# Positions of five mixer steps in a hand-ordered encoder layer (one core)

## The chip, the cores and the metric

One core of a Trainium2 chip runs the whole layer. The metric is the device time of one execution in microseconds (us). Engines in the profile's names: PE is the matrix engine (PEld its weight loads), DVE the vector engine, ACT the scalar engine, POOL the general-purpose engine whose queue issues some DMAs, SP the engine whose queue issues the weight loads.

## The reference, cut to what matters

One residual block over 256 tokens and a model width of 2048, in float32. "..." marks what is left out.

```
h = rms_norm(x, attn_norm_w)
hq, hf, hi, hg, c_q, c_kv, k_r = split(h @ w_in)      # 4 x 1024 and 512, 512, 64 columns
# head group A (8 heads of 128): gated linear recurrence
q = silu(hq);  f = lb + (1 - lb) * sigmoid(hf);  k = 1 - f;  b = cumsum(log f) inside chunks of 64
o_a = rms_norm(q . k . exp(b_t - b_s) against hi, plus the state carried over chunks) * silu(hg)
# head group B (8 heads): latent attention
q = rms_norm(c_q) @ w_uq;  kv = rms_norm(c_kv) @ w_ukv      # per head norm, rotary on 64 columns
o_b = softmax(mask(q k^T / sqrt(192))) v
x = x + concat([o_a, o_b]) @ w_out
...
x = x + (silu(gate) * up) @ w_down      # gate, up = rms_norm(x) @ w_gate_up, width 5632
```

## The kernel before, in words

**Granules.** All weights stream from HBM in pieces ("granules") of up to 128 x 1024 elements, in one fixed order. SP loads granule g into one of four slots of `raw` as soon as the old content of the slot has been split. ACT rounds it to `w_hi` (L793), DVE takes the difference `w_lo = raw - w_hi` (L1134), and PE multiplies it: tokens-high by `w_hi`, tokens-low by `w_hi`, tokens-high by `w_lo` (L1766, L1769), for two blocks of 128 tokens. A full granule of 2 x 512 columns is 12 matmuls of 512 columns; those of `w_uq` are 12 matmuls of 384 columns. The mixer has 137 granules. Their order is: three blocks of latent columns (granules 0 to 24), then hq 0 (25 to 32), uq 0 (33, 34), hf 0 (35 to 42), ukv 0 (43, 44), hi 0 (45 to 52), uq 1 (53, 54), hg 0, ukv 1, hq 1 (65 to 72), uq 2 (73, 74), ukv 2 (75, 76), hf 1 (77 to 84), uq 3 (85, 86), ukv 3 (87, 88), hi 1 (89 to 96), hg 1 (97 to 104), then w_out. The feed-forward part follows in loops of its own.

**Steps.** Everything else in the mixer is a *step*: an entry of the list that `schedule()` (L215) writes by hand, with a *position*, which is a granule's number. Each of PE, DVE and ACT walks the granules in order in its own instruction stream. At position g, PE first executes its part of the steps of g, then multiplies granule g (L1933). ACT and DVE first convert granule g + 3 and then execute their parts of the steps of g (L1061, L1680). Steps of one position keep the order in which the list names them. No engine reorders anything: whatever waits at the head of a stream holds back all that stands behind it, conversions too. A position is therefore an order within three queues, not a time.

**The steps that matter here.**
- `lat_in`, `lat_a`, `lat_b`, `swap lat`: normalize a latent (i = 0 for q, 1 for kv), transpose its 32 x 32 blocks on DVE, and let POOL's DMAs carry the blocks through HBM and back. `lat_t i n` splits the landed transpose: ACT writes `mT_hi` (L843), DVE then writes `mT_lo` (four instructions, L1155). Granule 33, the first of uq 0, waits for `lat_t 0 1`.
- `angles` (DVE, 19 small instructions, L1201 to L1225) and `sines` (ACT: it loads the table for Sin, waits for the angles, computes, and loads the next table, L866 and L832) make the rotary tables.
- `lb_a/b/c`: the lower bounds of the forget gate, on DVE and ACT. `kr_b`: rotation of the rotary key.
- `q_a`, `q_b`, `k_a`, `k_b`: squares of a block of heads on ACT (L815), mean on DVE, a root on ACT (L826, L828), scaling and rotation on DVE into `stage` (L1319, L1190 to L1195). `q_t`, `k_t`: PE transposes `stage` into two side banks (L1820, L1824) and ACT copies them out.
- `scores`, `softmax`, `probs_t`, `attend`: the attention of one head.
- `turn`: transposes of hq and hf; ACT writes `hqT`, `hkT` and the logarithms `logT` (L955). `scan g` is the cumulative sum on DVE (four instructions, L1374). `lev_a g l` makes the exponents of level l on DVE (L1386, L1387 for level 1), `lev_b` is two exponentials on ACT (L964, L965) and two products on DVE (L1405, L1406), `pairs g l` is PE's matmuls of the level (L1870 for level 1) and a masked copy on DVE.
- `o_a g`: PE computes the output of four heads in two side banks (L1913, L1914; 24 matmuls of 128 columns), ACT takes eight sums of squares (L815), DVE the mean (L1460). `o_b g`: a root on ACT, then DVE scales and gates the banks (eight instructions, L1470, four for each bank). `swap o 0`: transpose and DMAs as above.

**Side banks.** Four PSUM banks are dealt out in turn to all uses of PE's side work, in the order of the list: use n gets bank n modulo 4 (L1772), and PE waits until the use four before it has been read out:

```
pe.wait_ge(s_given[USES[n - SIDE][1]], GIVEN[n - SIDE])
```

A use of `o_a` counts as read out only by DVE's part of `o_b`. In the order before, the uses around it are: `attend 3` in bank 0, `q_t 2` in banks 1 and 2, `o_a 0` in banks 3 and 0, `k_t 2` in banks 1 and 2, `scores 4` in bank 3.

Of the kernel before, what the change touches and what calls it, by code (L numbers as in the profile page):

```python
# [101 lines left out]
END = {blk[:2]: 1 + max(g for g, x in enumerate(GRANULES) if x[0] == b) for b, blk in enumerate(BLOCKS)}  # L102
# [112 lines left out]
def schedule():  # L215

    s = [(FIRST, ("vec", 0))] + [(at, ("x", p)) for p, at in enumerate(X_TURNED)]  # L220
    s += [(2 * c + 3, ("sq1", c)) for c in range(4)]
    s += [(10, ("r1a",)), (11, ("r1b",)), (19, ("vec", 1))]

    s += [(END[("lat", n)] + 2 * (n == 0), ("lat_in", n)) for n in range(3)]
    for i in range(2):
        e = END[("lat", i + 1)]
        s += [(e + 1, ("lat_a", i)), (e + 2, ("lat_b", i)), (e + 2, ("swap", "lat", i))]
        s += [(e + 13 - 2 * i + n, ("lat_t", i, n)) for n in range(2)]
    e = END[("lat", 2)]
    s += [(e + 1, ("kr_a",)), (e + 4, ("angles",)), (e + 5, ("sines",)), (e + 9, ("kr_b",))]  # L230

    s += [(e + 7, ("lb_a", 0)), (e + 13, ("lb_b", 0)), (e + 15, ("lb_c", 0))]
    e = END[("ukv", 2)]
    s += [(e + 2, ("lb_a", 1)), (e + 3, ("lb_b", 1)), (e + 5, ("lb_c", 1))]


    for j in range(HEADS // 2):
        q, k = END[("uq", j)], END[("ukv", j)]
        early = j >= 2
        s += [(q - early, ("q_a", j)), (q - 1 if early else q + 1, ("q_b", j)), (q + 4, ("q_t", j))]  # L240
        early = j == 2
        s += [(k - early, ("k_a", j)), (k - 1 if early else k + 1, ("k_b", j)), (k + 4, ("k_t", j))]
        for h in (2 * j, 2 * j + 1):

            p = k + 5 + (j > 1) + (7 if j == 2 else 3) * (h % 2)
            s += [(p, ("scores", h)), (p + 1, ("softmax", h)), (p + 3 + (h == 6), ("probs_t", h)),
                  (p + 5 + (h in (4, 6)), ("attend", h))]

    for g in range(2):
        late = 5 * g  # L250
        e = END[("hf", g)]
        s += [(END[("hq", g)], ("hq", g)), (e - g, ("hf_a", g))]
        s += [(END[("hq", g)] + 1, ("swap", "hq", g))]
        s += [(e + 2 - 4 * g, ("turn", g, 0, t)) for t in range(NT)] + [(e + 3 + 3 * g, ("turn", g, 1, t)) for t in range(NT)]
        p = e + 5 + late
        s += [(p, ("scan", g))]
        for l in range(1, LEVELS + 1):
            s += [(p, ("lev_a", g, l)), (p + 1, ("lev_b", g, l)), (p + 4, ("pairs", g, l))]
            p += 4 if l == 1 else 3
        s += [(p + 1, ("join_a", g)), (p + 2, ("join_b", g)), (p + 5, ("join7", g)), (p + 6, ("join_c", g)),  # L260
              (p + 8, ("join8", g))]
        s += [(END[("hi", g)], ("hi", g)), (END[("hg", g)], ("hg", g))]

        p = max(p + 10, END[("hg", g)] + 2, END[("ukv", 2)] + 3)
        s += [(p, ("o_a", g)), (p + 1, ("o_b", g))] + [(p + 1, ("swap", "o", g))] * (g == 0)

        p = max(p + 4 - g, END[("ukv", HEADS // 2 - 1)] + 6)
        s += [(p, ("o_t", g, 0)), (p, ("o_t", g, 1))]

    for c in range(4):  # L270
        s += [(END[("out1", c)], ("out1", c)), (END[("out2", c)], ("out2", c)), (END[("out2", c)] + 1, ("sq2", c))]
    s += [(END[("out2", c)] + 2, ("x2", c, n)) for c in range(4) for n in range(2)]
    e = END[("out2", 3)]
    s += [(e + 3, ("r2a",)), (e + 4, ("r2b",))]
    return sorted(s, key=lambda x: x[0])


SCHEDULE = schedule()


# [1817 lines left out]
```

## Time and profile before

| | us |
|---|---|
| median of 3 runs (1129.71 to 1131.63) | 1129.92 |
| the profiled execution's own time | 1129.12 |
| its span, first to last instruction | 1127.4 |
| PE busy | 1112.1 (99% of the span) |
| PEld busy | 935.8 (83%) |
| DVE busy | 894.0 (79%) |
| ACT busy | 642.0 (57%) |
| mean granted PE clock | 0.998 of full |

The span is what the trace shows; 1.7 us of the execution's own time lie around it. A busy share is an average over the whole program; the change lies in the mixer, which is about the first 430 us. The sixteen DMA engines move 208 GB/s on average.

### The profile page before, as it was taken

Reading aid. Unit: us, or ns where it says so; the run is one execution under the profiler, and the core shown is the slowest. Engines: PE = TensorE matmul, PEld = TensorE weight load, DVE = VectorE, ACT = ScalarE, POOL = GpSimd, SP = SyncE. Lnnn points to the kernel's source line nnn. Section 1 sums busy time; section 2 is a strip of 40 time slices with the busy share of each in tenths; the row PEclk is TensorE's granted clock in tenths of the full one; section 3 lists DMA queues with packets and bytes.
Section 4 is the critical chain, followed back from the end, with each engine's and each line's share of the span. In section 5 each row is a group of like instructions: output and inputs, shape, how many; then the busy total and the mean of one; then the engine's idle time right before and its main releaser. Section 6 shows DMA issues by size and latency. Waiting matters only on the chain.

```text
span 1127.4 us, 15411 instructions
## 1 busy us (share of the span) xinstructions
PE 1112.1 (99%) x5225; PEld 935.8 (83%) x5225; DVE 894.0 (79%) x1217; ACT 642.0 (57%) x909; POOL 64.8 (6%) x159
## 2 busy tenths in 40 slices
PE   8999999999999999999999999999999999999998
PEld 7978888887888888888888888888888888888887
DVE  5679786588776567688888988988988879889777
ACT  7557866567764556454554554554554555555553
POOL 3010000010000000000010010010000010000000
PEclk9999999999999999999999999999999999999999
DMA  8687455556554455667677677677677786666665
GB/s 266 190 268 223 147 153 167 156 175 206 179 193 167 155 184 180 192 215 233 225 232 235 222 233 238 219 232 240 217 238 225 231 273 220 208 206 195 209 194 168
DMA packets 108919, 234.23 MB, mean 208 GB/s; under 512 B 8601, under 2 KB 19650, under 8 KB 108610
## 3 DMA queue, kind: packets, MB, share of 16 engines
q1 hardware_dynamic: 101346, 209.30, 58.0%
q0 software_dynamic: 7216, 24.12, 7.3%
q8 instruction: 29, 0.48, 0.2%
q14 instruction: 24, 0.20, 0.0%
q10 hardware_dynamic: 304, 0.14, 0.0%
HBM read 220.94 MB, written 12.58 MB: 207 GB/s over the span
## 4 chain that ended last, share of the span: by engine, by line
PE 90%; DVE 5%; ACT 2%; DMA 1%; issue 1%; POOL 0%; DVEq 0%; ACTq 0%; POOLq 0%; SPq 0%
PE side L1984 24%; PE main L1766 19%; PE side L1986 12%; PE main L1769 9%; PE side L1956 4%; PE side L1958 4%; PE side L1957 4%; PE main L1958 3%; PE main L1957 3%; PE main L1956 3%; DMA raw<-in_w_in 1%; DVE w_lo L1134 1%; PE side L1882 1%; PE side L1789 1%; ACT w_hi L793 1%
## 5 line engine op out<-in xcount | busy, mean ns | idle before, releaser
L1027 ACT CAST w_hi<-raw 128x1024 fp32r<-128x1024 f32 (+1 forms) x245 | 241.6, 990 | 173.0 <-PE side L1984 102.4
L1605 DVE TENSOR_TENSOR w_lo<-raw,w_hi 128x1024 fp32r<-128x1024 f32 (+1 forms) x245 | 275.5, 1139 | 22.3 <-ACT w_hi L1027 22.0
L1134 DVE TENSOR_TENSOR w_lo<-raw,w_hi 128x1024 fp32r<-128x1024 f32 (+3 forms) x156 | 178.4, 1153 | 105.5 <-ACT w_hi L793 103.4
L793 ACT CAST w_hi<-raw 128x1024 fp32r<-128x1024 f32 (+3 forms) x156 | 153.7, 993 | 139.8 <-PE main L1766 131.2
L1766 PE MATMUL main<-w_hi,hT_hi 128*128 128x512 f32 (+2 forms) x448 | 173.3, 388 | 2.1 <-DVE hT_lo L1155 0.9
L1769 PE MATMUL main<-w_hi,hT_lo 128*128 128x512 f32 (+2 forms) x448 | 169.1, 378 | 0.0
L1984 PE MATMUL side<-w_hi,hT_hi 128*128 128x512 f32 x400 | 155.6, 389 | 0.0
L1986 PE MATMUL side<-w_hi,hT_lo 128*128 128x512 f32 x400 | 155.6, 389 | 0.0
L1766 PE MATMUL main<-w_lo,hT_hi 128*128 128x512 f32 (+2 forms) x448 | 114.8, 378 | 0.0
L1984 PE MATMUL side<-w_lo,hT_hi 128*128 128x512 f32 x400 | 106.9, 389 | 0.0
L1766 PEld LDWEIGHTS main<-w_hi,hT_hi 128*128 128x128 f32 x448 | 84.8, 189 | 15.9 <-DVE hT_lo L1155 1.9
L1769 PEld LDWEIGHTS main<-w_hi,hT_lo 128*128 128x128 f32 x448 | 84.8, 189 | 13.0
L1766 PEld LDWEIGHTS main<-w_lo,hT_hi 128*128 128x128 f32 x448 | 83.0, 189 | 14.1
L1984 PEld LDWEIGHTS side<-w_lo,hT_hi 128*128 128x128 f32 x400 | 75.1, 188 | 15.6
L1984 PEld LDWEIGHTS side<-w_hi,hT_hi 128*128 128x128 f32 x400 | 75.1, 188 | 15.6
L1986 PEld LDWEIGHTS side<-w_hi,hT_lo 128*128 128x128 f32 x400 | 75.1, 188 | 15.6
L1984 PE MATMUL side<-w_hi,aT_hi 128*128 128x512 f32 x208 | 80.9, 389 | 0.0
L1986 PE MATMUL side<-w_hi,aT_lo 128*128 128x512 f32 x208 | 80.9, 389 | 0.0
L1605 DVE TENSOR_TENSOR w_lo<-last_two,w_hi 128x1024 fp32r<-128x1024 f32 x36 | 44.1, 1225 | 45.7 <-ACT w_hi L1027 45.7
L1027 ACT CAST w_hi<-last_two 128x1024 fp32r<-128x1024 f32 x36 | 37.9, 1052 | 59.9 <-PE side L1984 59.9
L1027 ACT CAST w_hi<-first_two 128x1024 fp32r<-128x1024 f32 x36 | 38.0, 1056 | 58.8 <-PE side L1984 58.8
L1766 PE MATMUL main<-w_hi,mT_hi 128*128 128x512 f32 (+1 forms) x160 | 62.7, 392 | 2.8 <-DVE mT_lo L1155 2.7
(293 smaller groups left out, 1836.0 us busy)
## 6 DMA issues: line engine op xcount, KB each, us to landing
raw<-in_w_gate_up SPq DMA_DIRECT2D x176, 512.0 KB, 4.8
raw<-in_w_down SPq DMA_DIRECT2D x88, 512.0 KB, 4.4
raw<-in_w_in SPq DMA_DIRECT2D x64, 512.0 KB, 4.4
raw<-in_w_out SPq DMA_DIRECT2D x32, 512.0 KB, 3.7
raw<-in_w_in SPq DMA_DIRECT2D x15, 384.0 KB, 4.4
squares<-hiddenT POOLq DMA_DIRECT2D x11, 512.0 KB, 5.2
hiddenT<-squares POOLq DMA_DIRECT2D x44, 128.0 KB, 4.9
raw<-in_w_ukv SPq DMA_DIRECT2D x8, 512.0 KB, 3.7
```

The lines of the kernel that those rows point to most:

```text
L793: copy(w_hi[:, slot, 0:n], raw[:, slot, 0:n]).then_inc(s_hi, 1)
L1027: copy(w_hi[:, n % RING, 0:cols], src).then_inc(s_hi, 1)
L1134: tt(w_lo[:, slot, 0:n], raw[:, slot, 0:n], w_hi[:, slot, 0:n].bitcast(F32), ALU.subtract)\
L1605: tt(w_lo[:, n % RING, 0:cols], src, w_hi[:, n % RING, 0:cols].bitcast(F32), ALU.subtract)\
L1766: m = matmul(banks[t][:, 0:cols], hi[:, at[n], tok], rhs, start=(part == "hi" and k == k_first), stop=(part == "lo" and k == last))
L1769: matmul(banks[t][:, 0:cols], lo[:, at[n], tok], rhs, start=False, stop=False)
L1789: m = transpose(ps[:, at:at + P], where[:, t, (k + n) * P:(k + n + 1) * P], ident[:, :])
L1956: matmul(bank, hi, big, start=first, stop=False)
L1957: matmul(bank, lo, big, start=False, stop=False)
L1958: return matmul(bank, hi, small, start=False, stop=last)
L1984: m = matmul(bank, hi, rhs, start=False, stop=(part == "lo" and (t, half) in last))
L1986: matmul(bank, lo, rhs, start=False, stop=False)
```

## The change

Five kinds of step get other positions; no instruction is added or taken away.

| step | position before | after |
|---|---|---|
| `lat_t 0 0`, `lat_t 0 1` | 30, 31 | 28, 29 |
| `scan 0`; `lev_a 0 1` | 48; 48 | 46; 47 |
| `o_a 0`; `o_b 0` and `swap o 0` | 80; 81 | 77; 78 |
| `scan 1`; `lev_a 1 1` | 95; 95 | 93; 94 |

`angles` stays at 29 and stands behind `lat_t 0 1` there; `sines` stays at 30. `scan 0` stands last at 46, behind `k_b 0` and the turns. At 78 `attend 3` stands ahead of `o_b 0`; at 79 stand `lb_a 1` and `q_t 2`. The side banks are dealt anew by the same rule: `o_a 0` gets banks 0 and 1, `attend 3` bank 2, `q_t 2` banks 3 and 0, `k_t 2` banks 1 and 2, `scores 4` bank 3.

```diff
     for i in range(2):
         e = END[("lat", i + 1)]
         s += [(e + 1, ("lat_a", i)), (e + 2, ("lat_b", i)), (e + 2, ("swap", "lat", i))]
-        s += [(e + 13 - 2 * i + n, ("lat_t", i, n)) for n in range(2)]
+        s += [(e + 11 + n, ("lat_t", i, n)) for n in range(2)]
...
         p = e + 5 + late
-        s += [(p, ("scan", g))]
+        s += [(p - 2, ("scan", g))]
         for l in range(1, LEVELS + 1):
-            s += [(p, ("lev_a", g, l)), (p + 1, ("lev_b", g, l)), (p + 4, ("pairs", g, l))]
+            s += [(p - (l == 1), ("lev_a", g, l)), (p + 1, ("lev_b", g, l)), (p + 4, ("pairs", g, l))]
             p += 4 if l == 1 else 3
...
-        p = max(p + 10, END[("hg", g)] + 2, END[("ukv", 2)] + 3)
+        p = max(p + 10, END[("hg", g)] + 2, END[("ukv", 2)])
         s += [(p, ("o_a", g)), (p + 1, ("o_b", g))] + [(p + 1, ("swap", "o", g))] * (g == 0)
```

## Rows read from the trace of the kernel before

**Rows 1.** PE's waits over the program: who, for whom, us in total, times, longest.

```profile
PE main L1766 <- DVE mT_lo L1155: 2.7, 1, 2.7
PE side L1870 <- DVE E L1406: 1.1, 1, 1.1
PE side L1843 <- DVE probs L1356: 0.8, 1, 0.8
PE main L1766 <- issue: 0.8, 1, 0.8
PE side L1833 <- DVE E L1470: 0.6, 1, 0.6
```

**Rows 2.** Timeline, PE, granules 32 to 39: start, us, engine, line, operation [idle before].

```profile
81.59 1.07 PE L1766 MATMUL main<-w_lo,hT_hi 128*128 128x512 f32 x4
85.31 0.45 PE L1766 MATMUL main<-w_hi,mT_hi 128*128 128x384 f32 x1 [2.65 <-DVE mT_lo L1155]
...
88.11 0.53 PE L1766 MATMUL main<-w_hi,mT_hi 128*128 128x384 f32 x1
...
102.08 0.60 PE L1820 MATMUL side<-ident,stage 128*128 128x128 f32 x4
```

**Rows 3.** Windows: stretch, PE, PEld, DVE, ACT, POOL busy, granted clock, DMA.

```profile
88.00:91.00 3.00, 3.00 (x13) 3.00 (x13) 1.58 (x3) 2.81 (x3) 0.00 (x0) 0.64 0.62 177
```

**Rows 4.** Timeline, DVE, positions 29 to 36.

```profile
80.63 0.95 DVE L1134 TENSOR_TENSOR w_lo<-raw,w_hi 128x768 fp32r<-128x768 f32 x1
...
84.12 1.13 DVE L1155 SCALAR_TENSOR_TENSOR mT_lo<-hbT,vec_cols,mT_hi 128x128 fp32r<-128x128 f32 x4
...
94.57 1.18 DVE L1134 TENSOR_TENSOR w_lo<-raw,w_hi 128x1024 fp32r<-128x1024 f32 x1
...
101.08 0.28 DVE L1195 TENSOR_TENSOR stage_r<-rot 128x128 f32<-128x128 f32 x1
```

**Rows 5.** Timeline, ACT, from `sines` to the end of `hq 0`.

```profile
81.09 1.28 ACT L832 ACT_TABLE_LOAD   x1
...
83.12 0.90 ACT L843 ACTIVATE mT_hi<-hbT,vec_cols 128x256 fp32r<-128x256 f32 x2
...
89.80 1.05 ACT L793 CAST w_hi<-raw 128x1024 fp32r<-128x1024 f32 x1
```

**Rows 6.** Timeline, PE, the first granules of the program.

```profile
6.41 0.52 PE L1769 MATMUL main<-w_hi,hT_lo 128*128 128x384 f32 x1
...
11.83 0.34 PE L1769 MATMUL main<-w_hi,hT_lo 128*128 128x384 f32 x1
```

**Rows 7.** Timeline, ACT, the last logarithm of `turn 0`.

```profile
128.18 0.59 ACT L955 ACTIVATE logT<-side 128x512 f32<-128x512 f32 x1
```

**Rows 8.** Timeline, DVE, from position 47 to `lev_a 0 1`.

```profile
131.25 2.36 DVE L1134 TENSOR_TENSOR w_lo<-raw,w_hi 128x1024 fp32r<-128x1024 f32 x2 [3.42 <-ACT w_hi L793]
133.53 2.43 DVE L1374 TENSOR_TENSOR_SCAN hbT<-keep,logT 128x256 f32<-128x256 f32 x4
...
136.65 1.22 DVE L1387 SCALAR_TENSOR_TENSOR E<-E,hbT 128x1024 f32<-128x1024 f32 x1
```

**Rows 9.** Timeline, ACT, conversions and the squares of `o_a 0` (the first of 8).

```profile
234.52 2.01 ACT L793 CAST w_hi<-raw 128x1024 fp32r<-128x1024 f32 x2
...
243.59 0.28 ACT L815 ACTIVATE junk<-side 128x128 f32<-128x128 f32 x1
...
246.72 1.04 ACT L793 CAST w_hi<-raw 128x1024 fp32r<-128x1024 f32 x1
```

**Rows 10.** Timeline, DVE, the scaling of `o_b 0`.

```profile
249.58 2.16 DVE L1470 SCALAR_TENSOR_TENSOR E<-side,stat,hgate 128x128 f32<-128x128 f32 x8
```

**Rows 11.** Timeline, PE: `q_t 2`, the end of `o_a 0`, the start of `o_a 1`.

```profile
234.63 0.60 PE L1820 MATMUL side<-ident,stage 128*128 128x128 f32 x4
...
240.94 0.39 PE L1914 MATMUL side<-hv,hS 128*128 128x128 f32 x2
...
378.95 1.05 PE L1914 MATMUL side<-hv,hS 128*128 128x128 f32 x8
```

## The prediction

> **What bounds the kernel now.** PE is busy for 99% of the span, so the change can win only where PE waits, and each new wait of PE costs its full length. I read the list of PE's waits first [rows 1]: 2.7 us for the low half of the first latent, once; 1.1 us for the products of level 1, once; 0.6 us for a side bank held by `o_b 0`; 0.8 us for the softmax of head 4; and 0.8 us under "issue". The timeline tells that the last is granule 89, the first of hi 1, whose main banks `q_b 3` reads late. All lie in the mixer. The timeline of PE then gives the pace: the four matmuls of the row at 81.59 take 1.07 us of which the last alone is 0.39, so 512 columns start every 0.227 us and a full granule takes 2.72 us; one of `w_uq` takes 2.08. What a side step costs PE is the distance between the main matmuls around it, less this pace: `q_t` or `k_t` 0.57, `attend` 0.58, `scores` 1.12, `o_a` 2.59, and the first main matmul behind any of them 0.11 more.
>
> The wait at 85.31 is dearer than it reads [rows 2]. PE stops for 2.65 us and resumes at full pace; 1.5 us later the pace halves, as the 0.53 us matmul at 88.11 shows, and the granted clock of the window from 88 to 91 is 0.64 of full [rows 3]: 1.2 GHz up to 90.1, 2.4 after. The two granules then take 5.84 us where 4.16 would do. So granule 35 starts at 91.15 instead of 86.65: 2.82 for the wait and 1.68 for the clock.
>
> **First latent's splits ahead of the angles.** In the changed order DVE does the first split after the conversion that ends at 74.87, the second after the next one. ACT has their high halves by 72.1 and 74.05; the transposed latent has landed before 70. Four L1155 instructions hold DVE 1.05 us [rows 4], so `angles` begins and ends 2.1 later, at 82.85 instead of 80.72. Behind it stands the conversion of granule 33, 80.63 before [rows 4], now 82.8 to 83.8. PE, which used to wait for the split, now waits for this conversion: 82.5 to 83.85, a wait of 1.3 where it was 2.8.
>
> What is late next is ACT. `sines` waits for the angles, then loads a table, 1.28 us [rows 5], and only then converts granule 34. That moves by +2.1; but the high half of the second split, 0.81 from start to start [rows 5], no longer stands behind it, so from granule 35's conversion on ACT is 1.4 late: the two tables and the Silu of `hq 0`, then granule 37's conversion at 91.2 instead of 89.80 [rows 5]. DVE waited 1.42 us for that one already, so all of its queue behind it moves by 1.4 too: `kr_b`, the transpose of hq, granule 38's conversion (94.57 before [rows 4], now 96.0 to 97.2), granule 39's, `lat_t 1 0`, and the rotation of `q_b 0`, whose last instruction starts at 101.08 [rows 4], now 102.5.
>
> PE meanwhile runs 33 from 83.85, 34 from 86.4 (its conversion), 35 from 88.5, 36, 37, and 38 from 97.2 (its conversion; 99.35 before). It reaches `q_t 0` at 100.0. Before, this began at 102.08 [rows 2], 0.7 after `stage` was ready; now it must wait until 102.85, a wait of about 2.8 us. Granule 39 starts near 103.4 instead of 102.65. The 4.5 us won at granule 33 are given back in full, and **+0.8** stays. The bounds: if ACT recovers its 1.4 us (it waits 0.6 for PE at 91.4) the term is 0; if a weight load lands late behind the later conversions it is +1.5.
>
> The clock: an idle stretch of 2.65 us cost 1.68 before [rows 2, 3]. The one ahead of `q_t 0` is as long, so I take **+1.6** again; the bounds are 0, if the clock stays up, and 2.5, from the start of the program, below. The old 1.68 at granule 34 is already in the +0.8.
>
> **Scan two places ahead, level 1 one place ahead, first group.** The last logarithm ends at 128.77 [rows 7], and DVE idles for 3.42 us up to 131.25 [rows 8]. `scan 0` at the end of position 46 falls into this hole: 128.85 to 131.3, its 2.43 [rows 8] at no cost. Then granule 50's conversion (to 132.45), `lev_a 0 1` (to 134.3 instead of 137.8 [rows 8]), conversions 51 and 52. PE needs the latter at 138.4 and 144, so nothing is late. The exponentials and products of `lev_b` end near 139, and PE arrives for `pairs` at 141.2: the wait of 1.1 [rows 1], 1.2 with its edges, is gone. A wait of 0.2 for the softmax of head 1, four positions on, goes too. Together **-1.4**, between -1.0 and -1.5.
>
> **The same in the second group.** PE's list names the level-1 products once only [rows 1], so the second `pairs` hardly waits: between -0.4 and +0.3 (the conversions of 97 to 99 now stand behind the scan, but have 2 us or more in hand). I take **-0.2**.
>
> **First output three granules ahead.** This is where I expect the loss. A use of a side bank waits for the use four before it. Now `q_t 2` at position 79 gets banks 3 and 0, and bank 0 is held by `o_a 0` until DVE's part of `o_b 0` at position 78 has read it. Before, the first to wait on such a bank was `scores 4` at 83, two positions after `o_b`, and even that waited 0.6 [rows 1].
>
> When is bank 0 free? PE does `o_a 0` at 228.2 to 230.8, which is 2.59 by the second `o_a` (378.95 [rows 11], main matmuls again at 381.54). But ACT is held until 233.65 by the root of `k_b 2`. It converts granule 80 from 234.52 [rows 9] to 235.5. Then come the eight sums of squares: 243.59 to 246.72 before, 3.13 us [rows 9], now 235.5 to 238.65. Then the conversion of 81 to 239.65, `attend 3` to 239.9, and the root of `o_b` to 240.4. DVE follows: conversion 81 from 239.7, `attend 3`, the reciprocal in three small instructions, and from 242.05 the scaling, 0.27 each of eight [rows 10]. Bank 0 is free after four, at 243.15.
>
> PE gets to `q_t 2` at 234.63 before [rows 11]. With 2.59 more and 0.1 less at `attend 3` it is there at 237.1, does its first bank by 237.55, and waits until 243.2: 5.6 us idle. Granule 79 starts at 243.4 and 80 at 246.2. Before, `o_a 0` ended and granule 80 started at 241.1 [rows 11]: 5.1 late. From this go the old waits that a later PE no longer meets: `scores 4` 0.65, `probs_t 4` 0.9, granule 89 1.0 (with the edges of the waits) [rows 1]. DVE and ACT are only 0.3 and 1.5 later by then, because lower bounds and conversions run while PE stands. That leaves **+2.5**. The bounds: +3.7 if the later ACT brings the third of these waits back and a load is late; and if bank 0 were free in time, -3.1: the three waits and the 0.5 us that `o_a 0` lost to `attend 3`.
>
> The clock again: 5.6 us is twice the idle time that sufficed. The Trainium skill (TensorE: Matmul & The Clock Gate, Part 1) puts it as "the default state is throttled, and activity releases the throttle". The trace agrees at the start of the program, which comes out of idleness: 384 columns start every 0.32 us from 6.41, and every 0.17 only from 11.83 on [rows 6], though the clock column shows full there. By the page alone the low level would hold from the restart on. Apart from that, the rows give two prices: 1.68 as at granule 34 [rows 2, 3], or half of the 5 us between the two rows of the start [rows 6], 2.5. I take **+2.1**, between 1.6 and 3.
>
> **The sum.** +0.8 + 1.6 - 1.4 - 0.2 + 2.5 + 2.1 = +5.4 against the profiled execution's own 1129.12, of which its span is 1127.4 and 1.7 lies around it unchanged: 1134.5. The median of the runs is 0.8 above that execution, so against 1129.92 it is 1135.3. I forecast **1135.2**.
>
> **The rivals.**
> *The clock stays up ahead of `q_t 0`, or at both places.* For it: one idle stretch of 2.65 is all the evidence, waits of 0.9 and 1.1 left the clock at full, and my 2.8 may come out at 2.2. Against: 5.6 us at `q_t 2`. One drop less gives 1133.6, none 1131.5.
> *`q_t 2` does not wait.* Place: bank 0. The other terms hold: +0.8 + 1.6 - 1.4 - 0.2 - 3.1 = -2.3, so 1127.6. It decides if the first four scalings are over by 237.6; the squares alone cannot end before 238.6 by the rows, so this needs ACT 5 us earlier than it can be.
> *The first move keeps its gain.* If `q_t 0` finds `stage` ready near 100 (ACT and DVE catch up 2.8 us), granule 39 is 2.7 early instead of 0.8 late and there is no drop of the clock: 5.1 less, 1130.1. With the last term at its lower clock price this touches no change, and only beyond that is it faster.
> *More is late.* A load behind the held conversions, or 3 us of lost clock at both places: 1138 to 1139.
> Should the steps win all that PE waits now and nothing wait anew, it would be -4.5 - 1.4 - 0.2 - 3.1, 1120.7. Bank and ACT speak against it.
>
> **How the numbers follow.** The forecast with both drops has 0.52; one or no drop 0.26; more is late 0.08; the first move keeps its gain 0.06; `q_t 2` does not wait, or all is won, 0.08. What a measurement here can tell from no change is 0.2%, 2.3 us. Faster takes the last case, 0.08; the same takes half of the one before it and the case without drops at its low end, 0.09; slower 0.83. The range 1131.2 to 1138.2 holds the first two cases and most of the third. The forecast's own range is 1133.4 to 1137.5.
>
> **What would show it.** In the changed trace: PE at 83 to 84 waits 1.3 us for a conversion, not for `mT_lo`; a wait of 2 to 3.3 us ahead of `q_t 0` near 100 to 103, released by L1195; no wait ahead of the first `pairs`; the scan right behind the last logarithm; and a wait of 5 to 6 us inside `q_t 2` (L1824) released by L1470, with matmuls of 0.53 us behind it. If L1824 does not wait there, the forecast is wrong in its largest step; if it waits and the total is still under 1131, the clock or the first move is.

## The result, and the profile after

The changed kernel takes **1132.36 us** (median of 20 runs, 1131.21 to 1134.69); the kernel before, run beside it, 1129.59 (20 runs, 1128.63 to 1131.63). The ratio is 1.0024, with a 95% interval from 1.0017 to 1.0031: 2.8 us slower. The forecast was 1135.2, 5.3 us slower than its 1129.92. The direction was right, and about half of the size came. One execution each of `e3_out` and `e4_qt81` below ran far slower than all others, 1574.38 and 1878.41 us at a mean granted clock of 0.67 and 0.56, and is left out of their ratios.

The profiled execution of the changed kernel is its slowest, 1134.69 with a span of 1133.0. PE is busy for 1113.3 us of it, where it was busy for 1112.1. PE's waits, in the form of [rows 1] (who, for whom: us in total, times, longest):

```profile
PE side L1824 <- DVE E L1470: 5.5, 1, 5.5
PE main L1766 <- DVE hT_lo L1155: 2.1, 1, 2.1
PE main L1766 <- DVE w_lo L1134: 1.9, 3, 1.0
PE side L1820 <- DVE stage_r L1195: 1.7, 1, 1.7
PE main L1766 <- issue: 1.1, 1, 1.1
```

All five waits of [rows 1] are gone: for `mT_lo`, for the products of level 1, for the softmax of head 4, at granule 89, and of `scores 4` for its bank. In their place stand the first row, inside `q_t 2`, and the last three, which lie between granules 33 and 39, but for 0.6 us of the row for `w_lo`, at 5.97 us. (Both kernels also wait 3.0 us at 3.0 us and 0.7 to 0.9 for their input, rows that neither list shows; the prediction's "all lie in the mixer" holds for the rows it names.)

The second row has nothing to do with the change. The wait ends at 16.73 us, where both kernels are the same program. The windows from 18 to 20 us (stretch, PE, PEld, DVE, ACT, POOL busy, granted clock, DMA), of the kernel before and of the changed one:

```profile
18.00:20.00 2.00, 2.00 (x15) 2.00 (x14) 1.56 (x3) 1.97 (x7) 0.44 (x1) 1.00 0.82 275
```
```profile
18.00:20.00 2.00, 2.00 (x10) 1.90 (x9) 1.62 (x5) 1.97 (x5) 0.85 (x1) 0.55 0.85 250
```

In this execution TensorE ran at half clock (1.2 instead of 2.4 GHz) from 18.2 to 21.6, and granule 5 starts 2.66 us later than before: 1.1 for the longer wait and 1.6 for the clock. So 2.66 of the 5.6 us between the two profiled executions are a chance of the start, and what is left, 2.9, is what the medians show (2.77). All that follows is net of the 2.66. The table says how much later than before the granules start (+) or earlier (-) through each place alone:

| place | granules | predicted | measured |
|---|---|---|---|
| first latent, rotation of `q_b 0` | 33 to 39 | +0.8 | +0.58 |
| clock ahead of `q_t 0` | 39 | +1.6 | 0 |
| `scan 0`, level 1 | 40 to 56 | -1.4 | -1.61 |
| first output, waits and later gains | 77 to 89 | +2.5 | +4.27, the next term in it |
| clock at `q_t 2` | 79 | +2.1 | 2.4 by its windows |
| `scan 1` | 99 | -0.2 | -0.36 |
| sum | | +5.4 | +2.9 |

The timeline of PE at the first place (start, us, engine, line, operation [idle before]), as [rows 2] showed it before:

```profile
86.37 0.41 PE L1766 MATMUL main<-w_hi,mT_hi 128*128 128x384 f32 x1 [1.04 <-DVE w_lo L1134]
...
88.98 0.41 PE L1766 MATMUL main<-w_hi,mT_hi 128*128 128x384 f32 x1 [0.29 <-DVE w_lo L1134]
...
92.42 0.47 PE L1766 MATMUL main<-w_hi,hT_hi 128*128 128x512 f32 x1 [1.09 <-issue]
...
105.26 0.66 PE L1820 MATMUL side<-ident,stage 128*128 128x128 f32 x4 [1.68 <-DVE stage_r L1195]
```

These are granules 33, 34 and 35 and `q_t 0`. The one wait of 2.65 became four, 4.10 in all. The clock stayed up behind all four; the window behind the last:

```profile
106.00:108.00 2.00, 2.00 (x11) 1.65 (x10) 2.00 (x6) 1.54 (x4) 0.00 (x0) 1.00 0.59 137
```

Granule 35 waits for nothing that the profile names ("issue"). ACT's timeline does name it:

```profile
87.01 2.74 ACT L793 CAST w_hi<-raw 128x768 fp32r<-128x768 f32 x3
89.76 1.28 ACT L938 ACT_TABLE_LOAD   x1
91.06 1.26 ACT L938 ACTIVATE lat<-main,stat 128x512 f32<-128x512 f32 x2
```

The Silu of `hq 0` (L938) reads the main banks that granule 35, the first of hf 0, writes anew. It ends at 92.32, and PE starts at 92.42. In the kernel before it was early enough, ending at 88.49, where granule 35 started at 91.15:

```profile
87.22 1.27 ACT L938 ACTIVATE lat<-main,stat 128x512 f32<-128x512 f32 x2
```

At the second place PE's timeline, as [rows 11] before:

```profile
238.75 0.60 PE L1820 MATMUL side<-ident,stage 128*128 128x128 f32 x4
244.83 0.69 PE L1824 MATMUL side<-ident,stage_r 128*128 128x128 f32 x2 [5.49 <-DVE E L1470]
...
245.74 0.63 PE L1769 MATMUL main<-w_hi,hT_lo 128*128 128x512 f32 x1
```

and what PE waits for, DVE's scaling of `o_b 0` ([rows 10] before):

```profile
243.65 2.16 DVE L1470 SCALAR_TENSOR_TENSOR E<-side,stat,hgate 128x128 f32<-128x128 f32 x8
```

Four of the eight, 0.27 each, end at 244.73, and PE resumes at 244.83. Behind it a matmul of 512 columns takes 0.63 us instead of 0.39, and four of them, from start to start, 1.7 instead of 0.91. The window says the same, clock 0.50:

```profile
246.00:249.00 3.00, 3.00 (x8) 2.32 (x8) 2.96 (x4) 0.30 (x1) 0.56 (x1) 0.50 0.17 70
```

The scan of the first group now fills DVE's hole, right behind the logarithm ([rows 7, 8] before), and `pairs` has no wait ahead of it. DVE's row, then PE's:

```profile
132.05 2.44 DVE L1374 TENSOR_TENSOR_SCAN hbT<-keep,logT 128x256 f32<-128x256 f32 x4 [0.97 <-ACT logT L955]
```
```profile
144.33 1.95 PE L1870 MATMUL side<-E 128*128 128x128 f32 x16
```

### The profile page after: what moved, and what is told of

Same layout as the page of the kernel before. It is cut to its first block, busy times and chain, and to the rows that moved or that the text cites. A ratio compares the mean times of both kernels' runs of the same rounds, so it can differ in the third digit from the quotient of the medians.

```text
span 1133.0 us, 15411 instructions
## 1 busy us (share of the span) xinstructions
PE 1113.3 (98%) x5225; PEld 937.3 (83%) x5225; DVE 894.6 (79%) x1217; ACT 641.7 (57%) x909; POOL 64.7 (6%) x159
## 4 chain that ended last, share of the span: by engine, by line
PE 92%; DVE 3%; ACT 2%; DMA 2%; issue 1%; ACTq 0%; DVEq 0%; SPq 0%
PE side L1984 24%; PE main L1766 20%; PE side L1986 12%; PE main L1769 10%; PE side L1956 4%; PE side L1957 4%; PE side L1958 4%; PE main L1957 3%; PE main L1958 3%; PE main L1956 3%; DMA raw<-in_w_in 1%; PE side L1882 1%; DVE w_lo L1134 1%; ACT w_hi L793 1%; PE side L1789 1%
```

## The experiments

Edits are against the kernel before unless said otherwise; each ratio is to that kernel's runs on the same chip.

**The three parts, each alone.** First the splits of the first latent:

```diff
-        s += [(e + 13 - 2 * i + n, ("lat_t", i, n)) for n in range(2)]
+        s += [(e + 11 + n, ("lat_t", i, n)) for n in range(2)]
```

> Only the first latent's splits are moved (positions 28, 29). Theory A (the 4.5 us won at granule 33 are spent again by granule 39, because ACT and DVE are later behind the angles): the wait for mT_lo and the low clock behind it are gone; in their place PE waits about 1.0 us for granule 33's conversion, 0.3 for granule 34's, 1.1 at granule 35 for the main banks that the Silu of hq 0 reads (under issue), and 1.7 ahead of q_t 0, all at full clock. Granule 39 starts 0.4 to 0.9 us later than before; time against the kernel before +0.3 to +1.0 us. Theory B (this move keeps most of its gain and the whole loss is elsewhere): -2 us or better, no wait ahead of q_t 0.

Measured: 1130.51 against 1129.54, ratio 1.0012 (1.0003 to 1.0021), +1.0. PE waits at the same places between granules 33 and 39 and as long as in the changed kernel; granule 39 starts 0.70 later than before, counted from granule 5. Its rows (0.5 of the first lies at the start of the program, and 0.8 of the second at granule 89):

```profile
PE main L1766 <- DVE w_lo L1134: 1.9, 3, 1.2
PE main L1766 <- issue: 1.9, 2, 1.1
...
PE side L1820 <- DVE stage_r L1195: 1.7, 1, 1.7
```

The move of the splits gives its whole gain back by itself, and no lost clock stands behind it: the clock is at full through the whole mixer in this profile, and ten of the eleven executions have a mean granted clock of 0.999 or 1.0.

Then scan and level 1:

```diff
-        s += [(p, ("scan", g))]
+        s += [(p - 2, ("scan", g))]
-            s += [(p, ("lev_a", g, l)), ...
+            s += [(p - (l == 1), ("lev_a", g, l)), ...
```

> Only the scan (two places) and the first level's arguments (one place) are moved, in both groups. Theory A: the waits at the first level's products of group 0 (1.1 us) and at the softmax of head 1 (0.2) are gone and a little in group 1, nothing new waits: -1.6 to -2.0 us. Theory B (the scan only pushes conversions, a wait comes back on a w_lo): between -0.5 and +0.5 us.

Measured: 1127.60, ratio 0.9985 (0.9976 to 0.9993), -1.9. The wait of L1870 is gone and none came in its place. This is inside what was expected. It is the one part of the change that helps.

Then the output alone:

```diff
-        p = max(p + 10, END[("hg", g)] + 2, END[("ukv", 2)] + 3)
+        p = max(p + 10, END[("hg", g)] + 2, END[("ukv", 2)])
```

> Only the first output is moved (o_a 0 at 77, o_b 0 at 78). Theory A (q_t 2 waits for the side bank that o_b 0 must read): PE waits 5 to 6 us at L1824 released by L1470, the clock is low for 4 to 6 us behind it, the old waits of 0.6, 0.8 and 0.8 go: +3.9 to +4.7 us. Theory B (the loss of the whole change is shared by its parts): +1 to +3 us.

Measured: 1134.48 (6 runs), ratio 1.0041 (1.0028 to 1.0054), +4.9, a little over what was expected. The wait is the same 5.5 us, and so is the clock behind it:

```profile
PE side L1824 <- DVE E L1470: 5.5, 1, 5.5
```
```profile
246.00:249.00 3.00, 3.00 (x8) 2.31 (x7) 2.70 (x4) 0.00 (x0) 0.55 (x1) 0.50 0.58 197
```

+1.0 - 1.9 + 4.9 = +4.0, against +2.8 for the whole. Each of the three is known to about 1 us, so this is within their intervals; the traces give +0.7 (`e1_lat`), -2.0 (the two scan rows of the table) and +4.3 (the output's row).

**Is it the bank?** The changed kernel, with `q_t 2` moved to position 81, where `o_b 0` has read the bank:

```diff
-        s += [..., (q + 4, ("q_t", j))]
+        s += [..., (q + 4 + 2 * (j == 2), ("q_t", j))]
```

> The whole change, with the transposes of the third pair of query heads (q_t 2) at position 81 instead of 79, so that they no longer stand in PE's queue ahead of granules 79 and 80 while o_b 0 still holds their bank; the banks are dealt as in the change. Theory A (the price is the bank wait at the head of PE's queue): the wait at L1824 shrinks from 5.5 to under 1 us, the clock stays at full, some of the old waits at head 4 come back: 4 to 6 us faster than the change, so -1 to -3 us against the kernel before. Theory B (the squares of o_a 0 on ACT and the scaling on DVE, pushed ahead of the conversions, are the price): PE waits for conversions instead, no more than 1.5 us faster than the change.

Measured: 1129.05 against 1129.54, ratio 0.9997 (0.9988 to 1.0006), 3.3 less than the changed kernel, where 4 to 6 less was expected. The wait for the bank fell from 5.5 to 0.7 and the clock is at 1.00 from 240 to 248. What is missing is in a new wait, at `scores 4`, for the copy of `k_t 2` on ACT, which now stands behind that of `q_t 2`:

```profile
243.98 0.63 PE L1820 MATMUL side<-ident,stage 128*128 128x128 f32 x4 [0.68 <-DVE E L1470]
...
252.25 0.49 PE L1833 MATMUL side<-X 128*128 128x128 f32 x2 [1.94 <-ACT kTr L910]
```

So the bank is the cause of the 5.5 us: `o_a 0`, its squares and its scaling stand where the change put them, and only the waiter has moved. Moving it costs 1.9 elsewhere.

The other way round: the kernel before with the output alone moved, and one position less far than in the change. `o_a 0` still stands ahead of `q_t 2`:

```diff
-        p = max(p + 10, END[("hg", g)] + 2, END[("ukv", 2)] + 3)
+        p = max(p + 10, END[("hg", g)] + 2, END[("ukv", 2)] + 1)
```

> The first output moved by two granules instead of three (o_a 0 at 78 behind attend 3, o_b 0 at 79), nothing else of the change. The banks are dealt otherwise by that: attend 3 in 0, o_a 0 in 1 and 2, q_t 2 in 3 and 0, k_t 2 in 1 and 2. Theory A (PE waits where a side use meets a bank of o_a): q_t 2 at 79 does not wait at all, k_t 2 at 81 waits 2 to 3.5 us for L1470 at full or partly low clock; +0.5 to +3.0 us. Theory B (the earlier output costs as such, by the work on ACT and DVE): +4 us or more, as with the move by three, and the wait is still in q_t 2.

Measured: 1129.56 against 1129.34, ratio 1.0002 (0.9993 to 1.0011). The banks are dealt anew: `q_t 2` waits for that of `attend 3`, and only `k_t 2` for `o_b 0`:

```profile
PE side L1824 <- DVEq L1160: 1.6, 1, 1.6
...
PE side L1820 <- DVE E L1470: 0.6, 1, 0.6
...
PE side L1824 <- DVE E L1470: 0.3, 1, 0.3
```

That there would be no wait inside `q_t 2` was wrong, and the total, +0.2, is under the low end of what was expected, 0.5. With the output one granule later in the list the loss of 4.9 is gone. Together with `e4_qt81`, where the output is as early as in the change, this says that the loss hangs on which use of a bank comes four behind, and not on how early the output is.

**What holds the gain of the first latent?** In all that follow, LAT stands for the edit of `e1_lat` and SCAN for that of `e2_scan`. First the angles and sines, which the splits now hold up, moved to positions 20 and 21:

```diff
+LAT, SCAN
-    s += [(e + 1, ("kr_a",)), (e + 4, ("angles",)), (e + 5, ("sines",)), ...
+    s += [(e + 1, ("kr_a",)), (e - 5, ("angles",)), (e - 4, ("sines",)), ...
```

> Splits, scan and first arguments as in the change, the first output left where it was, and the angles and sines at positions 20 and 21 instead of 29 and 30. Theory A (what spends the gain of the first move is the 4.7 us of angles on DVE and the two table loads on ACT ahead of granules 33 to 38): no wait at granules 33, 34, 35 nor ahead of q_t 0, the clock stays at full: -4.2 us for this place and -1.8 for the scan, so -5.5 to -6.5 us. Theory B (the Silu of hq 0 and the rotation are late anyhow): -2 to -3.5 us, with waits at granule 35 and q_t 0 left.

Measured: 1129.24 against 1129.34, ratio 1.0000 (0.9991 to 1.0009). Both expectations failed. ACT, in `sines` at 21, stood 4.59 us for the angles with the conversions behind it, and PE paid at granules 24 and 25, which in the kernel before have no wait at all:

```profile
61.73 0.38 PE L1766 MATMUL main<-w_hi,hT_hi 128*128 128x320 f32 x1 [2.27 <-DVE w_lo L1134]
...
64.96 0.47 PE L1766 MATMUL main<-w_hi,hT_hi 128*128 128x512 f32 x1 [1.23 <-DVE w_lo L1134]
```

One position between the two steps is too short for 19 instructions of DVE. From granule 33 to 38 PE no longer waited at all, but `q_t 0` still waited 1.6. Ahead of `stage` there is a chain of ACT and DVE that begins with granule 36's conversion (table, Silu of `hq 0`, table, two conversions, squares, root, scaling, rotation). In this run it took 16.7 us from the start of granule 33 to the ready `stage`, where PE takes 15.05 to come to `q_t 0`; in the changed kernel, where the angles hold ACT up, the same stretch is 18.8 (86.37 to 105.12). So 2.1 us of PE's stops behind the start of granule 33 are the price of the angles and sines, and 1.6 stay without them: what is won at granule 33 starts both PE and the chain sooner.

The same with the output at position 79, behind `q_t 2` (77 in the change, 80 before):

```diff
+LAT, SCAN, angles and sines as above
-        p = max(p + 10, END[("hg", g)] + 2, END[("ukv", 2)] + 3)
+        p = max(p + 10, END[("hg", g)] + 2, END[("ukv", 2)] + 2)
```

> As the kernel with the angles at 20, and the first output one granule ahead of the kernel before (o_a 0 at 79 behind q_t 2, o_b 0 at 80), where it keeps the banks that it had before. Theory A: the 0.5 us that o_a 0 lost to attend 3 stays or goes, the wait of scores 4 for the bank (0.65) goes, the softmax of head 4 comes up to 0.8 us earlier: 0.5 to 1.8 us faster than with the angles alone, -6.3 to -8 us in all. Theory B (the squares ahead of granule 83's conversion delay it): no faster than the angles alone.

Measured: 1132.36 against 1129.34, ratio 1.0025 (1.0016 to 1.0034), +3.0, where 6 to 8 less than before was expected. Beside the waits of `e5_angles` at granule 24 and `q_t 0` there is a new one, `o_a 0` for its second bank, which `attend 3` holds, and the clock falls behind it (0.62 of full from 238 to 241):

```profile
PE side L1913 <- DVEq L1160: 3.0, 1, 3.0
```

It was 0.2 us in the runs with `o_a 0` at 80.

If the chain is what holds, then `q_t 0` one position later should free PE of it, with the output back at 80 and the angles where they were:

```diff
+LAT, SCAN
-        s += [..., (q + 4, ("q_t", j))]
+        s += [..., (q + 4 + (j == 0), ("q_t", j))]
```

> Splits, scan and first arguments as in the change, the first output left where it was, the angles left where they were, q_t 0 at 40 instead of 39. Theory A (of the first move's price the 1.7 us ahead of q_t 0 are an order that can be mended; 2.4 us of waits at granules 33 to 35 stay): -2.6 to -3.4 us. Theory B (another step takes the wait's place behind it): -1 to -2 us.

Measured: 1126.99 against 1129.53, ratio 0.9978 (0.9968 to 0.9988), -2.5, just short of what was expected. The wait for `stage_r` is gone, and those at granules 33 to 35 are there (1.11, 0.27, 1.11).

With the angles at 13 and the sines at 17 as well:

```diff
+LAT, SCAN, `q_t 0` as above
-    s += [(e + 1, ("kr_a",)), (e + 4, ("angles",)), (e + 5, ("sines",)), ...
+    s += [(e + 1, ("kr_a",)), (e - 12, ("angles",)), (e - 8, ("sines",)), ...
```

> Splits, scan and first arguments as in the change, the first output left where it was; the angles at position 13, the sines four behind them at 17, where granules of 2.1 us leave both engines free; and q_t 0 at 40 instead of 39. Theory A (the run with the angles at 20 lost its gain to two waits for conversions behind the angles, because ACT stood waiting in sines, and to 1.6 us ahead of q_t 0, which the Silu of hq 0 and its two table loads alone explain): at most 1 us of new waits at granules 16 to 18, none from 33 to 40: -4.5 to -6 us. Theory B (moving the angles only moves the wait): -1 to -3 us, with 2 us or more of waits for w_lo at granules 16 to 20.

Measured: **1125.11** against 1129.53 (6 runs), ratio 0.9961 (0.9948 to 0.9974), -4.4, just short of the 4.5 to 6 expected. This is the best of all: 4.4 us under the kernel before and, with each taken against the kernel before, 7.2 under the changed one. After granule 0 PE waits for no `w_lo` any more; of its waits between granules 33 and 40 this one, at granule 35, is left:

```profile
87.75 0.47 PE L1766 MATMUL main<-w_hi,hT_hi 128*128 128x512 f32 x1 [0.38 <-issue]
```

Against `e10_qt40` the angles' place is worth 1.9 by the medians and 2.4 by the start of granule 39.

Last, the "issue" wait of granule 35, with the Silu of `hq 0` one position earlier:

```diff
+LAT
-        s += [(END[("hq", g)], ("hq", g)), (e - g, ("hf_a", g))]
+        s += [(END[("hq", g)] - (g == 0), ("hq", g)), (e - g, ("hf_a", g))]
```

> The first latent's splits alone at 28 and 29, and the Silu of hq 0 one position earlier (32), ahead of ACT's conversion of granule 36, nothing else. Theory A (the 1.1 us wait at granule 35 is for the main banks that this Silu reads, and what PE waits there it no longer waits ahead of q_t 0): the wait at granule 35 is under 0.3 us, the one ahead of q_t 0 grows from 1.7 to 2.5 to 2.9 us, granule 39 starts as before within 0.3; the time is that of the splits alone where the clock stays up and 1.6 us more where it falls. Theory B (the two are separate): the wait at granule 35 goes, that at q_t 0 stays 1.7 or less, 1 us faster than the splits alone.

Measured: 1131.89 against 1129.53, ratio 1.0017 (1.0008 to 1.0026). The wait of granule 35 fell from 1.1 to 0.17, which shows that the Silu caused it. In its place came 0.69 at granule 36, for `w_lo`, whose conversion now stands behind the Silu, and 0.2 more ahead of `q_t 0`:

```profile
93.07 0.47 PE L1766 MATMUL main<-w_hi,hT_hi 128*128 128x512 f32 x1 [0.69 <-DVE w_lo L1134]
...
103.39 0.66 PE L1820 MATMUL side<-ident,stage 128*128 128x128 f32 x4 [1.90 <-DVE stage_r L1195]
```

Neither expectation came as written (the wait at `q_t 0` grew by 0.2, not by 0.8 to 1.2), but the sum of its stops, 4.27, is that of the four of the splits alone, 4.23. So the overlooked wait is not a loss of its own. With the splits early and the angles at 29, PE reaches `q_t 0` only when the chain to `stage` is through; what it does not wait on the way, it waits there. Here the clock fell behind the 1.90 (its row is at the end), and in six of the eleven executions: those have a mean granted clock of 0.998 and lie at 1131.89 to 1132.76, the five with 0.999 or 1.0 at 1130.05 to 1131.09.

**What the clock does after a short idle.** The wait ahead of `q_t 0` made longer, by moving the splits of the second latent ahead of the rotation (35 and 36 instead of 36 and 37):

```diff
-        s += [(e + 13 - 2 * i + n, ("lat_t", i, n)) for n in range(2)]
+        s += [(e + 11 - i + n, ("lat_t", i, n)) for n in range(2)]
```

> As the kernel with the first latent's splits alone at 28 and 29, and besides the second latent's splits one place ahead (35 and 36 instead of 36 and 37), so that one more split of 1.05 us stands in DVE's queue ahead of the rotation that q_t 0 waits for. Theory A (my prediction's step on the clock failed only because the wait ahead of q_t 0 came out at 1.7 us instead of 2.8, part of it having been taken at granule 35): the wait at L1820 is 2.6 to 3.0 us, the clock falls to the low level behind it and costs 1.6 us more, so 2.3 to 3.2 us slower than the splits alone, +3.3 to +4.2 us against the kernel before. Theory B (the clock does not fall at this place, whatever the wait): the wait grows by 1.05 and the time by just that, +2.0 to +2.3 us.

Measured: 1133.32 (5 runs, 1132.13 to 1133.98) against 1129.34, ratio 1.0037 (1.0023 to 1.0051). The wait is 2.7 us, the length that was predicted for the change. The profiled execution is the fastest of the five, and in it the clock stayed at full (mean 1.0; the other four have 0.998). One more execution of the same kernel:

> The same kernel as the one with the second latent's splits one place ahead (wait ahead of q_t 0 of 2.7 us, profiled at full clock at 1132.1, while its timed runs lay at 1133.2 to 1134.0). Theory A (a wait of 2.7 us brings the clock down in most executions and not in all): 1133 to 1134 with matmuls at half pace behind q_t 0. Theory B (it never falls here): full pace behind q_t 0 again.

Measured: 1133.07, and this time it fell. The windows behind the wait, first of `e7_late_rotation`, then of `e12_again`:

```profile
106.00:107.50 1.50, 1.50 (x8) 1.23 (x7) 1.47 (x3) 0.55 (x2) 0.00 (x0) 1.00 0.44 137
```
```profile
106.00:107.50 1.50, 1.50 (x5) 1.18 (x4) 1.47 (x3) 0.46 (x2) 0.00 (x0) 0.50 0.53 167
```

Counted from granule 5, granule 40 starts 1.81 us later than before in the first and 3.37 in the second: 1.56 for the clock, about the price that the prediction took. With the long wait there, the fall came in five of the six executions and cost what was forecast; what was missing in the change is the long wait, not the price.

## Why the prediction was half right

**The step that failed is "The clock: [...] The one ahead of `q_t 0` is as long, so I take +1.6 again."** It rests on PE stopping for some 2.8 us ahead of `q_t 0`. Counted as the prediction counts them, from the end of one granule's pace to the next start, its stops of PE are 1.4 at granule 33, 0.5 at 34, 0.5 at 38 and 2.8 at `q_t 0`, 5.2 in all. Counted in the same way, the changed kernel has 1.2, 0.5, then 1.4 at granule 35, none at 38, and 1.8 at `q_t 0`, 4.9 in all (4.10 as the profile gives idle time). So the sum was near, and with it the term of +0.8 (measured +0.58). The place was not. The prediction had itself put the Silu of `hq 0` 1.4 us later, which makes its end 89.9 instead of 88.49, and let PE start granule 35 at 88.5; it never checked the one against the other, though this granule needs the banks that the Silu reads. PE stopped there for 1.09, and that left 1.68 of idle time ahead of `q_t 0` in place of 2.8.

Behind this shorter stretch the clock stayed at full in the changed kernel's profile and in that of `e1_lat`, and in nearly all other executions. The result of each execution names its mean granted clock. A low stretch of 3.4 us, as at the start in the profiled one, takes 0.0015 off it, and that around `q_t 2`, 6.9 us (243.5 to 250.4), takes 0.003; a mean of 0.999 or 1.0 leaves no room for a whole short one. Of the changed kernel's 20 executions 18 have 0.997 or 0.998, which is the fall at `q_t 2` alone; two have 0.995, room for one more: the profiled one, where it is the fall at the start, and the next slowest, 1134.09. The rival "the clock stays up ahead of `q_t 0`" gave 1133.6, and held 0.26 together with no fall anywhere; it is the case that came. The bounds of the term, 0 to 2.5, did hold the truth. That a wait of 1.7 leaves the clock up is not a certainty either but what most executions did; the numbers are at the end.

The other 0.9 is in small sizes, all on the same side: 0.2 at each of the first latent, `scan 0` and `scan 1`, and 0.3 at the output.

**The first output** was right in each of its steps: the bank, the holder, the wait (5.6 predicted, 5.49 measured), the fall of the clock (2.1 against 2.4), and the waits given back later: granule 80 is 7.66 later by this place, and the net at 89 is 4.27, so 3.4 came back, where the prediction had 2.6 of old waits. Shown by `e3_out`, which has this part alone, and by `e4_qt81` and `e8_out78`, where another use of the bank removes it.

**The scans** were right, their gain a little larger than forecast (2.0 against 1.6); the hole in DVE hides all of the 2.44 us. Shown by `e2_scan`.

**"ACT is late next"** was right about the chain and was confirmed by the two runs that go around it, `e10_qt40` and `e9_early_angles`. That `sines` and the angles were all that made it late was my theory after the result, and `e5_angles` showed it to be half true: with them out of the way PE does not wait from granule 33 to 38, and the wait ahead of `q_t 0` is still 1.6.

**The 4.5 us "won at granule 33"** had little to gain at granule 39 even without a later chain, which the prediction does not say. In the kernel before, PE came to `q_t 0` only 0.7 after `stage` was ready, so with the chain where it was no more than 0.7 was to be won there (an estimate from these two times). The falls of the clock at granule 33 say the same: of the 76 executions of the kernel before that ran beside the experiments, 26 have a mean clock of 0.999 or 1.0, without room for a whole one, and their medians are only 0.4 to 0.6 us lower than those of the executions at 0.998, though the fall makes granule 35 1.68 later.

What stays open: why 13 of the changed kernel's 20 runs lie within 1131.2 to 1132.6 and seven up to 2.1 us above. Two of the seven are those with 0.995. The other five have the same mean clock as the 13, and part of their distance lies outside the span (2.0 to 2.9 us around it, against 1.7 to 2.4); no run says why. And `e9_early_angles` was not combined with a better place for the output.

## What to carry to other kernels

When a step is moved ahead in a queue with banks dealt out in turn, redo the deal and ask for every bank who holds it and in which queue its release stands: here one position more or less turned 0 to 5 us of wait around. What is won upstream of a chain in other queues is lost again where PE waits for that chain; measure the chain (16.7 us against PE's 15.05) first, and move the waiter (`q_t 0`, one position) if it can go. When a step on ACT is made later, look for every granule that needs what it reads or writes, main banks too. List idle time by stretch and not only in total: four stretches of 0.3 to 1.7 us cost no clock in the changed kernel, while one of 2.7 cost 1.6 more in five of six executions.

## What the chip showed that was not expected

Whether TensorE falls from 2.4 to 1.2 GHz after a short idle stretch differs between executions of one kernel. In the profiles:

| idle stretch, us | the clock stayed up | the clock fell |
|---|---|---|
| 1.68 | changed kernel and `e4_qt81`, `q_t 0` | |
| 1.8 to 1.9 | start of `e10_qt40`, `e11_hq32`, `e12_again` | `e11_hq32`, `q_t 0` |
| 2.0 to 2.1 | start of `e4_qt81` | start of the changed kernel |
| 2.27, granule 24 | `e5_angles` | `e6_both` |
| 2.5 to 2.65, granule 33 | | before, `e2_scan`, `e3_out`, `e8_out78` |
| 2.74, `q_t 0`, one kernel | `e7_late_rotation` | `e12_again` |
| 2.99 | | `e6_both`, `o_a 0` |
| 5.5 | | changed kernel and `e3_out`, `q_t 2` |

By the mean clocks of all executions it fell in one of 11 with 1.7 ahead of `q_t 0` (`e1_lat`), in six of 11 with 1.9 and in five of six with 2.7, as far as each has no other fall, which a mean can't tell. A fall cost about 1.6 us behind the short waits and 2.4 behind the long one. It did not always begin with the restart: in the kernel before 1.5 us behind it, at `q_t 2` in the changed one 1.3 us ahead of it. The row of `e11_hq32` behind its 1.90:

```profile
106.00:108.00 2.00, 2.00 (x6) 1.52 (x6) 1.97 (x3) 0.00 (x0) 0.00 (x0) 0.50 0.85 253
```

The row of `e6_both` behind its 2.27 at granule 24, where a matmul of 320 columns takes 0.47 us:

```profile
61.77 0.47 PE L1769 MATMUL main<-w_hi,hT_lo 128*128 128x320 f32 x1
```

So a difference of 2 to 3 us between two single profiles means nothing here until the falls of the clock in both are counted. The start alone, the same in every kernel, was 0 to 0.9 us later than before in the profiles of the twelve experiments and 2.66 in that of the changed kernel.
